# Residual joins of a two-layer decoder step: the last chunk and the residual update by halves of the tokens

## The reference, cut to what matters

```
def _rmsnorm(x, g):
    y = x * rsqrt(mean(x * x, axis=-1) + 1e-6)
    return y * g
x = x + _rmsnorm(mixer(_rmsnorm(x, pre)), post)
x = x + _rmsnorm(ffn(_rmsnorm(x, pre2)), post2)     # ffn: (silu(gate) * up) @ w_down
```

## Time and profile before

| | us |
|---|---|
| median of three executions | 2893.11 |
| lowest, highest | 2881.28, 2901.33 |
| the profiled execution, its own time | 2919.01 |
| its span | 2917.2 |
| TensorE busy | 2704.7 |
| VectorE, ScalarE, GpSimd busy | 1351.6, 993.8, 1243.8 |
| products of line L652 on the chain | 65% of the span |

### The profile page before, as it was taken

The page is one execution under the profiler, slowest core; times in us unless marked ns, Lnnn a source line. Parts: engine busy times, 40 slices in busy tenths (PEclk is TensorE's granted clock), DMA queues, the critical chain, the costliest instruction groups (busy, mean ns, idle before and its releaser), DMA issues.

```text
span 2917.2 us, 44626 instructions
## 1 busy us (share of the span) xinstructions
PE 2704.7 (93%) x15729; PEld 2393.5 (82%) x15733; DVE 1351.6 (46%) x1820; ACT 993.8 (34%) x1450; POOL 1243.8 (43%) x632
## 2 busy tenths in 40 slices
PE   7979667999999979999987899999999989999998
PEld 5669535888887768888866679999999979999997
DVE  3449765799698554312345523220234443220234
ACT  3241454432233344322235524222223334222222
POOL 4434223455454335555545304543443334543441
PEclk9979878999999999999988869999999999999998
DMA  4444210233332212333321121232232211232231
GB/s 125 98 121 89 78 50 19 65 101 101 90 107 84 66 51 74 99 101 94 99 81 62 43 64 57 80 91 75 79 89 63 80 48 57 81 93 73 81 93 52
DMA packets 451745, 230.09 MB, mean 79 GB/s; under 512 B 90588, under 2 KB 443568, under 8 KB 451127
## 3 DMA queue, kind: packets, MB, share of 16 engines
q1 hardware_dynamic: 451647, 228.80, 27.2%
HBM read 213.43 MB, written 15.43 MB: 78 GB/s over the span
## 4 chain that ended last, share of the span: by engine, by line
PE 80%; DVE 11%; ACT 3%; issue 3%; POOL 2%; DMA 1%; SPq 0%; DVEq 0%; ACTq 0%; POOLq 0%
PE psum L652 65%; PE psum L684 3%; PE psum L751 2%; DVE top L1765 2%; DVE scores L1772 1%; DVE scores L1910 1%; PE psum L956 1%; PE psum L784 1%; PE psum L946 1%; PE psum L768 1%; DVE probs_t L1975 1%; PE psum L963 1%; DVE row_stats L1966 1%; PE psum L1012 1%; POOL act_split L1600 1%
## 5 line engine op out<-in xcount | busy, mean ns | idle before, releaser
L652 PE MATMUL psum<-act_split,w_hi 128*128 128x288 f32 (+1 forms) x6144 | 1364.5, 331 | 33.0 <-POOL w_lo L1568 11.6
L1568 POOL TENSOR_TENSOR w_lo<-w_raw,w_hi 128x1024 fp32r<-128x1024 f32 (+1 forms) x336 | 860.3, 2561 | 1248.3 <-ACT w_hi L1144 1248.3
L652 PEld LDWEIGHTS psum<-act_split,w_hi 128*128 128x128 f32 x6144 | 994.9, 190 | 128.2 <-issue 19.2
L1144 ACT ACTIVATE w_hi<-w_raw 128x1024 fp32r<-128x1024 f32 (+1 forms) x336 | 376.8, 1122 | 1394.6 <-PE psum L652 1371.0
L652 PE MATMUL psum<-act_split,w_lo 128*128 128x288 f32 (+1 forms) x3072 | 842.2, 329 | 0.0
L652 PEld LDWEIGHTS psum<-act_split,w_lo 128*128 128x128 f32 x3072 | 526.4, 190 | 40.8
L652 PE MATMUL psum<-hidden_split,w_hi 128*128 128x288 f32 (+1 forms) x2112 | 461.4, 327 | 0.0
L652 PEld LDWEIGHTS psum<-hidden_split,w_hi 128*128 128x128 f32 x2112 | 339.4, 188 | 27.4
L652 PE MATMUL psum<-hidden_split,w_lo 128*128 128x288 f32 (+1 forms) x1056 | 287.6, 327 | 0.0
L2034 DVE TENSOR_TENSOR temps<-psum,root_of_input 128x512 f32<-128x512 f32 (+1 forms) x88 | 63.4, 721 | 356.0 <-PE psum L652 344.9
L2040 DVE TENSOR_TENSOR temps<-psum,temps 128x512 f32<-128x512 f32 (+1 forms) x88 | 63.3, 719 | 350.7 <-PE psum L652 332.4
(11 more groups left out here) (250 smaller groups left out, 2495.7 us busy)
## 6 DMA issues: line engine op xcount, KB each, us to landing
w_raw<-in_w_ffn_gate_up SPq DMA_DIRECT2D x352, 256.0 KB, 3.1
w_raw<-in_w_ffn_down SPq DMA_DIRECT2D x64, 384.0 KB, 3.6
w_raw<-in_w_ffn_down SPq DMA_DIRECT2D x64, 320.0 KB, 4.1
w_raw<-in_w_in_even SPq DMA_DIRECT2D x64, 256.0 KB, 3.7
w_raw<-in_w_in_odd SPq DMA_DIRECT2D x64, 256.0 KB, 3.0
w_raw<-in_w_out_odd SPq DMA_DIRECT2D x32, 256.0 KB, 3.0
x_rows<-in_x_prompt SPq DMA_DIRECT2D x8, 512.0 KB, 6.2
w_raw<-in_w_out_even SPq DMA_DIRECT2D x32, 128.0 KB, 2.9
```

The costliest lines, as they stand in the source:

```text
L652: mm = pe.matmul(PS[:, 2 * p + b, 0:hi - lo], w[:, p, at], x(k)[:, lo:hi], start=(k == 0 and w is WH and x is x_hi), stop=(k == ph.kt - 1 ...
L1144: act.activation(WH[:, p, 0:n], WR[:, p, 0:n], ACT.Copy).then_inc(S("w_hi"), 1)
L1568: pool.tensor_tensor(WL[:, p, 0:n], WR[:, p, 0:n], WH[:, p, 0:n].bitcast(F32), ALU.subtract).then_inc(S("w_lo"), 1)
```

## The change

All eight joins are rewritten. The last chunk of the phase ahead of a join (`last_chunk`) runs over half the columns of the tokens (`HT` = 256 or 288) and then over the other half, with the sums, the root and the spread of half 0 inside the products of half 1. The residual update is done in units: four blocks of half 0, four of half 1, then three whole blocks, then the last block by halves (`UNITS`, `STEPS`). TensorE runs the first chunk of the next phase unit by unit; the second chunk lags, since VectorE now copies its high part and GpSimd subtracts its low part within the join. GpSimd adds the squares of two units, and TensorE sums the pairs. The `hold` products are gone. In join 3 the first two token tiles are transposed after half 0. The large selection round behind the last pair of `dn` moves behind the third pair of `v`. The rounds on the sample scores stand three per block from the first block on. Cells of `RT` and tiles of sums follow the halves (four in group 0, six in group 1). The waits for key and value pages of the sample attention become one. Renumbered semaphores and changes that only follow from these are left out here, as are blank lines; eight columns of indent are taken off.

```diff
+UNITS = [(0, k) for k in range(4)] + [(1, k) for k in range(4)] + [(BOTH, k) for k in (4, 5, 6)] + [(0, 7), (1, 7)]
+NU = len(UNITS)
+STEPS = [(h, k) for h, k in UNITS[:8]] + [(h, k) for k in (4, 5, 6) for h in (0, 1)] + UNITS[11:]
+STEP_END = (1, 2, 3, 4, 5, 6, 7, 8, 10, 12, 14, 15, 16)
...
+    def last_chunk(ph, x_hi, x_lo, s):
+        g, i = ph.g, ph.iters - 1
+        j = 4 * g + s
+        e = ph.free[1]
+        pe.wait_ge(S("w_lo"), ph.c0 + 2 * ph.iters)
+        pe.wait_ge(S(f"free_{e}1"), ph.base[e, 1] + i)
+        for h in (0, 1):
+            for k in range(ph.kt):
+                at = slice(P * k, P * k + P)
+                for w, x in ((WH, x_hi), (WH, x_lo), (WL, x_hi)):
+                    mm = pe.matmul(PS[:, 2 + h, 0:HT[g]], w[:, 1, at], x(k)[:, part(h, g)],
+                                   start=(k == 0 and w is WH and x is x_hi),
+                                   stop=(k == ph.kt - 1 and w is WL))
+                if h and k == ph.kt // 3:
+                    half_sums(g, s, 0)
+                if h and k == 2 * ph.kt // 3:
+                    pe.wait_ge(S("n_rc"), r_at(g, SPOST[s]) + 1)
+                    spread(0, g).then_inc(S("n_b"), 1)
+            mm.then_inc(S("w_used") if h else S("last_a"), 1)
...
+    def half_sums(g, s, h):
+        j = 4 * g + s
+        if h:
+            pe.wait_ge(S("n_rt"), r_at(g, SPOST[s]) + 1)
+        pe.wait_ge(S("ss_last"), 2 * j + h + 1)
+        for k, lo, w in cells(h, g):
+            mm = pe.matmul(PS[0:w, 7, 2 * k:2 * k + 1], SS[:, lo:lo + w], ONES[:, 0:1], start=True, stop=True)
+        mm.then_inc(S("n_sum"), 1)
...
+        def products(p, h, k, parts):
+            at = slice(P * k, P * k + P)
+            for w, x in parts:
+                for b in ((0, 1) if h == BOTH else (h,)):
+                    mm = pe.matmul(PS[:, 2 * p + b, 0:HT[g]], w[:, p, at], x(k)[:, part(b, g)],
+                                   start=(k == 0 and w is WH and x is a_hi),
+                                   stop=(k == NB - 1 and x is a_lo))
+            return mm
+        first, second = ((WH, a_hi), (WL, a_hi)), ((WH, a_lo),)
+        def second_chunk(h, k):
+            return products(1, h, k, first + second)
+        def sums(u, sem, value):
+            pe.wait_ge(S(sem), value)
+            add_sums(square_at(u, g), UNITS[u][0], g).then_inc(S("sq_used"), 1)
+        pair_free(ph, 0)
+        at = split_at(2 + 4 * g + (0, 1, 3)[s])
+        for u, (h, k) in enumerate(UNITS):
+            pe.wait_ge(S("a_hi"), at + u + 1)
+            products(0, h, k, first)
+            pe.wait_ge(S("a_lo"), at + u + 1)
+            mm = products(0, h, k, second)
+            if u == NU - 1:
+                mm.then_inc(S("w_used"), 1)
+            if u == 1:
+                half_sums(g, s, 1)
+            if u == 3:
+                pe.wait_ge(S("n_rc"), r + 2)
+                spread(1, g).then_inc(S("n_b"), 1)
+            if u == 4:
+                open_sums(g)
+                sums(0, "sq_pair", 5 * m + 1)
+                pair_free(ph, 1)
+                second_chunk(0, 0)
+            if u == 5:
+                sums(2, "sq_pair", 5 * m + 2)
+                second_chunk(0, 1)
+            if u == 6:
+                second_chunk(0, 2)
+                second_chunk(1, 0)
+            if u == 7:
+                sums(4, "sq_pair", 5 * m + 3)
+                second_chunk(0, 3)
+            if u == 8:
+                sums(6, "sq_pair", 5 * m + 4)
+                second_chunk(1, 1)
+            if u == 9:
+                second_chunk(1, 2)
+                second_chunk(1, 3)
+            if u == 10:
+                sums(8, "sq_pair", 5 * m + 5)
+            if u == 11:
+                sums(10, "sq_m", NU * m + 11)
+        second_chunk(BOTH, 4)
+        sums(11, "sq_m", NU * m + 12)
+        second_chunk(BOTH, 5)
+        sums(12, "sq_m", NU * m + 13)
+        close_sums(g).then_inc(S("n_sum"), 1)
+        second_chunk(BOTH, 6)
+        pe.wait_ge(S("n_rc"), r2 + 1)
+        spread(BOTH, g).then_inc(S("n_b"), 1)
+        second_chunk(BOTH, 7).then_inc(S("w_used"), 1)
...
-        ph = (phase("out", g), phase("dn", g, 0, 1), phase("oo", g), phase("dn", g, 1, 1))[s]
-        pe.wait_ge(S(f"free_{ph.free[0]}0"), ph.end[ph.free[0], 0])
-        block_sums(norm_at("post", g, s), g, 2)
-        hold(2)
-        spread(r_at(g, SPOST[s]), g)
-        hold(5 if s < 3 else 3)
...
+        half_sums(g, 3, 1)
+        pe.wait_ge(S("n_rc"), r_at(g, SPOST[3]) + 2)
+        spread(1, g).then_inc(S("n_b"), 1)
...
                 if k == 0:
-                    pe.wait_ge(S("x_new"), 8 * (4 * g + 3) + n + 1)
+                    pe.wait_ge(S("x_new"), 16 * (4 * g + 3) + n + 1)
+                if k == 2:
...
+    def last_block(g, s, h):
+        ph = (phase("out", g), phase("dn", g, 0, 1), phase("oo", g), phase("dn", g, 1, 1))[s]
+        j, e = 4 * g + s, ph.free[1]
+        square = PS[:, 6 - h, 0:HT[g]]
+        if s in (0, 2):
+            act.wait_ge(*((S("w_used"), ph.c0 + NB) if h else (S("last_a"), j + 1)))
+            act.activation(square, PS[:, 2 + h, 0:HT[g]], ACT.Square).then_inc(S("sq_last"), 1)
+            act.activation(Y[:, NB - 1, part(h, g)], PS[:, 2 + h, 0:HT[g]], ACT.Copy).then_inc(
+                S(f"free_{e}1") if h else S("y_a"), 1)
+        else:
+            act.wait_ge(*((S(f"free_{e}1"), ph.end[e, 1]) if h else (S("y_a"), j + 1)))
+            act.activation(square, Y[:, NB - 1, part(h, g)], ACT.Square).then_inc(S("sq_last"), 1)
...
-        root(r_at(g, SPOST[s]), g)
+        j, m = 4 * g + s, 3 * g + s
+        last_block(g, s, 0)
+        act.wait_ge(S("n_sum"), r_at(g, SPOST[s]) + 1)
+        root(0, g).then_inc(S("n_rt"), 1)
         if s == 3:
+            last_block(g, s, 1)
+            act.wait_ge(S("n_sum"), r_at(g, SPOST[s]) + 2)
+            root(1, g).then_inc(S("n_rt"), 1)
+            if g == 0:
+                hi_part(phase("out", 1), 0, 1)
             return
-        m = 3 * g + s
-        for n in range(NB):
-            base, layer = ((G_FFN_PRE, 0), (G_MIX_PRE, 1), (G_FFN_PRE, 1))[s]
-            act.wait_ge(S("x_new"), 8 * (4 * g + s) + n + 1)
-            act.activation(AR[:, 0, n, 0:T[g]], X[:, n, 0:T[g]], ACT.Identity, scale=gain(base, layer, n)).then_inc(S("a_hi"), 1)
-            act.activation(Y[:, n, 0:T[g]], X[:, n, 0:T[g]], ACT.Identity, scale=gain(base, layer, n)).then_inc(S("z_in"), 1)
-            if n >= 2:
-                act.wait_ge(S("sq_used"), 8 * m + n - 1)
-            act.activation(SQ[:, n % 2, 0:T[g]], X[:, n, 0:T[g]], ACT.Square).then_inc(S("sq_m"), 1)
-        root(r_at(g, SPRE[s]), g)
+        base, layer = ((G_FFN_PRE, 0), (G_MIX_PRE, 1), (G_FFN_PRE, 1))[s]
         nxt = (phase("gu", g), phase("v", g), phase("gu", g, 1))[s]
+        def square(u):
+            h, n = UNITS[u]
+            wait(act, S("sq_used"), 8 * m + (0 if u < 8 else 2 if u < 10 else 4))
+            act.activation(square_at(u, g), X[:, n, part(h, g)], ACT.Square).then_inc(S("sq_m"), 1)
+        for u, (h, n) in enumerate(UNITS):
+            act.wait_ge(S("x_new"), 16 * j + STEP_END[u])
+            act.activation(AR[:, 0, n, part(h, g)], X[:, n, part(h, g)], ACT.Identity, scale=gain(base, layer, n)).then_inc(S("a_hi"), 1)
+            act.activation(Y[:, n, part(h, g)], X[:, n, part(h, g)], ACT.Identity, scale=gain(base, layer, n)).then_inc(S("u_gx"), 1)
+            if u == 0:
+                last_block(g, s, 1)
+            else:
+                square(u - 1)
+            if u == 2:
+                act.wait_ge(S("n_sum"), r_at(g, SPOST[s]) + 2)
+                root(1, g).then_inc(S("n_rt"), 1)
+        square(NU - 1)
         act.wait_ge(S("w_used"), nxt.c0 + 1)
         hi_part(nxt, 1, 0)
+        root_all(r_at(g, SPRE[s]), g)
         act.wait_ge(S("n_b"), r_at(g, SPRE[s]) + 1)
-        act.activation(RB[:, 0:T[g]], PSF[:, 2048:2048 + T[g]], ACT.Copy).then_inc(S("rb"), 1)
+        act.activation(two(RB[:, 0:T[g]], g), PS[:, 4:6, 0:HT[g]], ACT.Copy).then_inc(S("rb"), 1)
     def gate(g):
         ph = phase("v", g)
...
-        if s == 3:
-            return
-        for n in range(NB):
-            split(a_at_(g, SA_[s]), n, g, Y[:, n, 0:T[g]], 3 * g + s)
+        m = 3 * g + s
+        nxt = (phase("gu", g), phase("v", g), phase("gu", g, 1))[s]
+        def low(u):
+            h, n = UNITS[u]
+            at = part(h, g)
+            pool.wait_ge(S("u_gx"), NU * m + u + 1)
+            pool.tensor_tensor(AR[:, 1, n, at], Y[:, n, at], AR[:, 0, n, at].bitcast(F32), ALU.subtract).then_inc(S("a_lo"), 1)
+        def weights(half):
+            at = slice(512 * half, 512 * half + 512)
+            pool.wait_ge(S("w_hi"), nxt.c0 + 2)
+            ins_ = pool.tensor_tensor(WL[:, 1, at], WR[:, 1, at], WH[:, 1, at].bitcast(F32), ALU.subtract)
+            if half:
+                ins_.then_inc(S("w_lo"), 1)
+        def add(u):
+            pool.wait_ge(S("sq_m"), NU * m + u + 2)
```

(91 more changed lines are left out.)

326 lines of the change are left out of this document (168 added, 158 removed).

## The result

The changed kernel takes 2928.09 us, median of 4 runs (2921.38 to 2955.87), beside 2896.09 for the kernel before (4 runs): ratio 1.0124, 95% interval 1.0077 to 1.0171. Timed again on another chip (6 runs), it was 2930.22 beside 2894.04: 1.0108, 1.0081 to 1.0134. It is slower by some 32 us, at or just past the 1% (29 us) taken as the border of no change, and 19 us above the forecast of 2909.

A forecast was written before the change was run, and what follows sets the result against it. TensorE was taken as the bound nearly everywhere outside sparse attention. Inner joins +9.4, clock +13.2, outputs -7.7 and small things +1 gave +16 us on a profiled 2919.0, or 2909 us against the median; own range 2890 to 2922, full range 2860 to 2933.

The forecast's parts named there:

- slower rival: Clock falls in the joins' sparse front and again amid one-column sums, in at least three joins: 2932 us; chance 0.22.
- Front: Join's start, before dense products: first product 5.3 us earlier, then an ordered chain between engines until L+15.6.
- L: The moment half A, the first token half of the last chunk, is complete; 2.6 us before the old chunk end in g0.
- first rival: At the inner joins the front costs nothing because the chain to half B's spread is overlapped: 2863 us; chance 0.25.
- Inner joins: The six joins leading into a first pair of weight chunks: 214.8 against 205.4 us, +9.4 before the clock.
- clock term: TensorE's clock falls 7 us after L in the six inner joins: +1.6 per g0 join, +2.8 per g1 join, +13.2 us.
- Outputs: The two output joins, with fewer transpositions behind the last half step: -4.2 us in g1, -3.5 in g0, together -7.7.
- Small things: Six instead of five tiles in g1's other sums and spreads, and one wait for both page sets: +1 us.
- moved selection round: Large selection round moved into the value stage, covered by the last pair's products: costed at nothing, up to 7.8 us without cover.
- Weight copy: Copy VectorE takes over from ScalarE in the inner joins: 0.75 us, covered by VectorE's 4 us of idle front.
- possible lock: VectorE's weight copy waiting for or blocking GpSimd over SBUF: at most 4.8 us over six joins, taken as 0.
- 5.3 and 3 come back, 12 go into the front: Balance of g0's third join in us, ending in a loss of 3.5 us for that join.

The follow-up runs named there:

- Experiment 2: Changed kernel with half B's sums, root and spread issued one or two units earlier; ratio 1.0076 to the kernel before.
- second profile: Changed kernel timed and profiled again with no edit, on another chip; 2930.22 us, ratio 1.0108 to the kernel before.
- experiment 6: Changed kernel with half B's statistics issued early, plus filler products in the gaps of the six inner joins' front; ratio 1.0026 to the kernel before.
- experiment 4: Kernel before without its filler products in all eight joins, nothing else changed; ratio 1.0136 to the kernel before.
- experiment 1: Kernel before with the change made at the two output joins alone; ratio 1.0003, in two groups of times.
- kernel 8: Kernel before with the change at the two outputs only, plus 12 filler products where the sample sequences' attention begins; 2885.99 us, ratio 0.9956.
- kernel 10: Kernel before with only the 12 filler products at the start of the sample sequences' attention; ratio 1.0003.
- kernel 9: The kernel of experiment 6 with two blocks of the second chunk's products moved later among the last sums; ratio 1.0047 to the kernel before.
- kernel 7: Changed kernel with the second weight chunk not lagging from the fifth unit on; ratio 1.0126 to the kernel before.
- Kernel 11: The code of kernel 9 plus the 12 filler products in the attention; ratio 1.0033 to the kernel before.

## Why the prediction came out as it did

The mechanism of the front was right, and so was the sign. That the time lay in the range says little: 2928 is 19 us above the forecast, outside the forecast's own range (2890 to 2922), and nearer to the slower rival's 2932, whose condition was not met in the first profile. It was inside because the range was drawn wide enough to take in both rivals.

**Front.** Its whole order was seen. Forecast and measured in g0's third join, after L: first residual step 3.1 and 4.0; first product 4.7 and 5.7; reciprocal of half B 9.1 and 9.5; its spread done 12.7 and 13.7; fifth unit's low part 15.6 and 16.5; end 35.0, or 36.6 with the clock, and 36.0. The first product stands 4.3 us nearer to the old chunk end than before (5.3 in the forecast's working, some 4 in its list of signs). The 0.9 us at the start is the ordinary add ahead of half A's: 2.51 us long, it ended 1.3 us after L, and I had let half A's own add start without it. VectorE's idle hole was 3.27 us (forecast 4), GpSimd's work 17.4 (22.18 in the window, less two ordinary weight parts of 2.4; forecast 18.4). Experiment 2 shows that the hole is the written order. The first rival (a front that costs nothing) falls with it.

**Inner joins.** Forecast +9.4 and +13.2 for the clock, 22.6; measured +25.4 in the profile, +36.1 in the second one. The sum hides two misses that offset each other. g0's first join took 33.4 us where 38.0 was forecast, because VectorE was not 4.6 us late there: its ordinary additions between the selection rounds took 0.7 us and not 2.1, and the last one ended 1.3 us after L. g1's second took 47.6 where 39.4 was forecast. The other four came within 0.8 us. Low stretches came close to where I put them (L+9.4 to L+23.1 in g0's third, forecast L+7 to L+20.5; 17.1 us long in g1's first and third), and experiment 6 gives the clock term by medians as 15. The split between order and clock is not settled by that: the six joins have 84 us more at the low level than before, and at the 0.39 us of experiment 4 they alone would be 33 us, more than the whole loss. What I gave a chance of 0.22, a second fall, came true in one join of the first profile (g1's second: 23.9 and 17.1 us, +10.8) and in two of the second; in g0's second join the clock fell twice as well in both profiles, both times in the front and not amid the sums. It stayed short of the three joins that the rival needed, but it explains why the joins lost more than the forecast.

**Outputs.** -7.7 forecast, -7.8 in experiment 1; the changed kernel's own g1 output gave 2.8 and 3.6.

**Small things: the term that failed.** I took +1 for the sixth tile and the merged page wait. The input and value stages took 9.3 us more, 11.0 in the second profile, with 24 and 28 us more at clock 0.50. Together they took 768.3 to 771.5 us in the five profiles with old inner joins and 776.3 to 782.5 in the eight with new ones, so the increase goes with the new code. Which of its edits makes it was not tested, and that it came through the clock is argued from the low us alone. These vary without the change too: kernel 1, with the old code there, had 47 us low in the first input stage (39 before, 48 after), kernel 8 had 37. The g1 value stage took 140.9 to 142.3 us in the five profiles with old joins (before, 1, 4, 8, 10) and 143.3 to 146.5 with the new ones. The moved selection round cost little: g0's value stage grew 0.4 us (2.8 in the second profile, with 11 us more at the low level).

**Weight copy.** It took 0.71 us (0.75 estimated), but the forecast's cover for it was not there: it stands ahead of VectorE's third pair and on the chain of waits (1136.48, 0.71 us), while the idle hole comes after the fourth pair. So part of the front's delay is this copy. No lengthening by the possible lock shows, though GpSimd hardly ran beside it (its low parts stand at 1135.92 and 1137.28, 0.72 and 0.73 us long).

**Against the old joins.** What I did not see is how much the old filler was worth. I read 1.00 in two joins and priced its loss within the new joins only. Experiment 4 puts 39 us on it. The rule of the Trainium skill that the prediction weighed (page "TensorE: Matmul & The Clock Gate", section "HAM oscillation — how this bites in real kernels": bursts with waits between pay the restart each time) speaks the same way, and the traces agree, 179 us at clock 0.50 in the six joins against 43. The change drops that, and by timed runs earns back only 3 to 8 us of the 39 in the whole kernel, outputs included. So the loss of the filler is by itself at least as large as the whole slowdown, and "5.3 and 3 come back, 12 go into the front" set the new join against a filled old one only.

**Open.** Kernels 6 and 9 have joins about as long as those of before in their profiles (+3.6 and -5.1 us), and a g1 output some 2 us shorter, yet they are 0.3 and 0.5% slower. For kernel 6 the profile of kernel 10 closes the gap: against it the joins are 7.0 us longer, the input and value stages 7.2, g0's output with the attention 2.7 shorter, g1's output 2.9 shorter, together 8.7 of the 9 us between the medians. For kernel 9 the same sum gives 4 of 13 us; its profile was the fastest of its six runs, and the rest lies in runs without a profile.

## To carry to other kernels

When a boundary is split in halves to overlap it, issue the second half's statistics as soon as its data is there: here a root, a sum and a spread placed one or two units too late in two queues left VectorE waiting 3.3 us in a join and cost 9 to 14 us by timed runs (20 in one pair of profiles), though GpSimd was not the bound. Before filler products are dropped, take them out alone and time that; and put filler into gaps before the clock falls, not on the path after it. Halving paid at the outputs, where little follows, and not at the joins that lead into a dense first pair of products.

## What the runs showed of the hardware

- Dense work does not by itself bring the clock back soon. In the sample sequences' attention TensorE was 100% busy from 1670 to 1710 at clock 0.50, and the low level lasted 68 us in the profile of before (1662.7 to 1731.0). With twelve filler products of 256 columns in two idle gaps at its start (1.5 and 1.7 us) the clock read 1.00 there in the profile of kernel 8, and none of its 11 runs was in the upper group, while 6 of 12 runs of kernel 1, on another chip, were.
- A low microsecond cost 0.39 us on average over six joins (52 for 135, kernel 4 against before); the longer low time of g1's third join in the second profile of the changed kernel, amid dense products, cost 0.43 each (8.7 for 20.4).
- The steady rate of TensorE is not quite constant. In kernel 7 the same 3006 products of one feed-forward stage took 2% less than those of another, at a granted clock of 1.00 and 0.99:

```profile
1816.60:2218.10 401.50, 401.50 (x3007) 401.50 (x3007) 106.03 (x78) 101.39 (x118) 180.42 (x79) 1.00 0.28 83
2493.20:2885.90 392.70, 392.70 (x3008) 392.70 (x3007) 106.00 (x78) 101.25 (x118) 180.09 (x79) 0.99 0.28 82
```

Kernel 11 had such a stage too, 391.7 us against 401.7 for the same products, at 1.00 both times. Nothing in the profiles says why; 9 us in one stretch is as much as many edits are worth.
